# Moving modulation weights out of two feed-forwards into the mixers

## The chip, the cores and the metric

The kernel runs on one core of one Trainium2 chip. The metric is the device time of one execution in microseconds (us), median of several runs. The kernel before takes 2105.08 us (three runs, 2104.85 to 2108.06).

## The reference, cut to what matters

Two transformer blocks of two layers each run one after the other over 256 tokens of width 1024, all in float32. Each layer has a mixer (projections, attention and, in the first block, a state space scan) and a feed-forward (SwiGLU of width 2816, or eight experts). That makes eight stages, numbered m = 0 to 7; stage 3 is the one with the experts. Ahead of each stage its input is shifted and scaled, and behind it the result is gated, by vectors that depend on the condition `c` alone:

```
m = einsum("bd,de->be", silu(c), w) + b          # w: 1024 x 3072 for every stage
shift, scale, gate = split(m, 3)
h = norm(x) * (1 + scale) + shift                # the stage's input
x = x + gate * stage(h)                          # second block; a layer norm around it in the first
```

So each stage needs three thirds (j = 0 shift, 1 scale, 2 gate) of its own 12 MB matrix, and they can be computed at any time before the stage needs them.

## The kernel before, in words

**The ring.** All large weights come in blocks of 1 MB (128 partitions x 2048 floats) through a ring of six slots (`NS = 6`). `plan` is the order of the blocks, 517 in all. The SyncE queue (SP) issues the loads strictly in that order (L2987, `load`), and load n waits until block n - 6, which had the slot before, has been used. A weight block of a stage is split by ScalarE (ACT) into a high half (`high_halves`, L1263, `ring_hi`, three buffers) and by VectorE (DVE) into a low half in the ring slot itself (`low_halves`, L1960, `ring_lo`), and TensorE (PE) makes three products of it (L499 to L501). `ahead(i)` says how far ahead of block i the halves are made: two blocks, but across the border to the next stage only one, the first block of that stage.

**The modulations.** A block `("mod", m, j, p)` is a quarter (p = 0 to 3) of one third. Only DVE uses it: two multiply-adds into `acc` or another accumulator (L1900, `gemv`). DVE takes the quarters off the list `mods_left` in the order of the plan, in `low_halves`, before it makes the low half of the first weight block that stands behind them. `together(m)` adds up shift and scale over the partitions on PE (L550) just before the stage, and takes what is left of them first.

**The order around the change.** `weave` spreads modulation blocks evenly between the blocks of a feed-forward. The first feed-forward (m = 1) carries 32 of them, among them shift and scale of stage 3; the second mixer (m = 2) four; the third mixer (m = 4, `mixer2(0)`) eight, one behind each block from the ninth on; the third feed-forward (m = 5) 28, among them all of stage 7; the last mixer (m = 6, `mixer2(1)`) and the last feed-forward (m = 7) none. "The third feed-forward" is here the one of the second block's first layer, which stands behind the experts.

**The end of a mixer.** A mixer's 16 blocks are 12 of the input projection and four of the output projection, `wout2` 2, 3, 0, 1 in this order. PE uses `wout2` 2 and 3 during the attention, and 0 and 1 in `last_blocks`, whose 48 products end the mixer; the signal that block 0 has been used is given six products before the last. ACT's last steps are `out_block(0)` and `out_block(1)`, and DVE's are `block("wout2", 0)` and `block("wout2", 1)`. The last one makes the halves of the first block of the next feed-forward, `w1 0 0`. Both engines work in order, so only behind it do they come to `rms_rows` and `rms_boundary`: the residual (L2044, L2049), the sum of squares, the normalized rows, which PE transposes (L581) and which give the next stage's input. `mixer1` ends in the same way, with `wout` 2 and 3 taken whole (`whole_block`, L888) and `outputs` (L2371, L2376) and `mixed` (L2037) before it.

Of the kernel before, what the change touches and what calls it, by code (L numbers as in the profile page):

```python
# [87 lines left out]
def hybrid_kernel(nc, a, out):  # L88
    ctx = ExitStack()
    with ctx:  # L90
# [251 lines left out]
        def put_blocks(blocks):  # L342
            for b in blocks:
                block(*b)
# [4 lines left out]
        for i, n in enumerate((0, 1, 1, 1, 1, 2, 2)):  # L349
# [8 lines left out]
                         mods((1, 2), (4, 0), (4, 1), (2, 0), (2, 1), (2, 2), (3, 0), (3, 1))))  # L358
        put_blocks(weave(win_blocks(1) + rowblocks(("wout", 1), a["w_out"][1]), mods((3, 2))))
# [4 lines left out]
        for l in range(2):  # L364
            win2 = [(("win2", l, i), (kview(8, 256), krows(a["w_in_2"][l][:, 256 * i:256 * i + 256]))) for i in WIN2]
            blocks = win2 + rowblocks(("wout2", l), a["w_out_2"][l])
            for i, b in enumerate(blocks):
                put_blocks([b] + (mods((5, 0), (5, 1))[i - 8:i - 7] if l == 0 and i >= 8 else []))
            put_blocks(weave(ffn_blocks((("ffn2", l), a["w_gate_2"][l], a["w_up_2"][l], a["w_down_2"][l])),
                             mods((5, 2), (6, 0), (6, 1), (6, 2), (7, 0), (7, 1), (7, 2)) if l == 0 else []))  # L370

        split = [key for key, _ in plan if key[0] != "mod" and key not in WHOLE]
        turn_of = {key: i for i, key in enumerate(split)}
# [873 lines left out]
        def scalar_program(act):  # L1247
# [335 lines left out]
            def mixer2(l, m):  # L1583
                M = ("m2", l)

                def project(i, dst, *waits, at_once=False):
                    summed(turn_of["win2", l, i])
                    if not at_once:
                        high_halves(main, ahead(turn_of["win2", l, i]))
                    act.wait_ge(*at(*M, "proj", i))  # L1590
                    for z in waits:
                        act.wait_ge(*at(*z))
                    act.activation(dst, R2.of(*M, "proj", i)[:, :].rearrange("p (t c) -> p t c", t=2), ACT.Copy).then_inc(
                        *main.act((*M, "projected", i), ("free", *M, "proj", i)))
# [59 lines left out]
                project(10, vt(2), at_once=True)  # L1654
                values_in(2)
                turn_group(0)
                halves_for(10)
# [220 lines left out]
        def vector_program(dve):  # L1878
# [71 lines left out]
            def low_halves(s, upto):  # L1950

                while done[0] <= upto:
# [8 lines left out]
                    done[0] += 1  # L1961

# [221 lines left out]
            def mixer1(l, m):  # L2184
# [238 lines left out]
                late_features()  # L2423
                outputs()
                mixed(M, range(2), "wout", l, None)
# [3 lines left out]
            def mixer2(l, m):  # L2429
# [120 lines left out]
                mixed(M, range(2), "wout2", l, evac)  # L2550
                block("wout2", 0)
# [557 lines left out]
```

## Time and profile before

| | us |
|---|---|
| median of three runs | 2105.08 |
| lowest, highest | 2104.85, 2108.06 |
| the profiled execution's own time | 2110.58 |
| its span (first to last instruction) | 2108.7 |
| PE busy (share of the span) | 1979.9 (94%) |
| DVE busy | 1673.0 (79%) |
| ACT busy | 1170.4 (56%) |
| mean granted TensorE clock | 0.96 |

The profiled execution is 5.5 us above the median of the runs, and its span is 1.9 us shorter than its time. Differences inside the span can be set against the median as they are. A busy share is a mean over stages that have different limits, so the stages are to be read one by one.

### The profile page before, as it was taken

How to read it: one execution, taken by the hardware profiler on the slowest of the kernel's cores; microseconds unless marked ns; L12 is line 12 of the kernel's file. 1: busy time of each engine (PE TensorE's matmuls, PEld its weight loads, DVE VectorE, ACT ScalarE, POOL GpSimd, SP SyncE). 2: the span in 40 equal slices, each digit the busy share in tenths (PEclk: the TensorE clock that was granted, in tenths of full speed). 3: DMA queues.
4: the chain of work that ended last, by engine and by line, in shares of the span. 5: the costliest groups of instructions: out<-in, count | busy, mean ns of one | idle time of the engine just before them, and what ended most of it. 6: DMA issues, size and time to landing. Idle time of an engine off the chain costs nothing.

```text
span 2108.7 us, 28332 instructions
## 1 busy us (share of the span) xinstructions
PE 1979.9 (94%) x11530; PEld 1713.3 (81%) x11530; DVE 1673.0 (79%) x1753; ACT 1170.4 (56%) x1316; POOL 72.4 (3%) x121
## 2 busy tenths in 40 slices
PE   6989999999799999999999999878899999989999
PEld 6778899886678887887878888668689989869998
DVE  6777889887788998989898888878778886756444
ACT  3544334464567777777777777556444344654432
POOL 6001000000000000000000000000010000000000
PEclk9988999899899999999999999989789998989999
DMA  9754999644499999999999999824359994324552
GB/s 350 267 183 162 349 352 361 215 150 162 166 343 335 352 373 343 341 358 370 324 356 365 361 336 349 310 81 159 120 209 355 353 366 134 121 80 140 180 182 98
DMA packets 251210, 554.37 MB, mean 263 GB/s; under 512 B 10077, under 2 KB 75857, under 8 KB 251073
## 3 DMA queue, kind: packets, MB, share of 16 engines
q1 hardware_dynamic: 247252, 544.13, 72.3%
q0 software_dynamic: 3552, 8.29, 1.2%
q8 instruction: 94, 1.54, 0.3%
q14 instruction: 44, 0.35, 0.1%
q10 hardware_dynamic: 268, 0.07, 0.0%
HBM read 551.40 MB, written 1.05 MB: 262 GB/s over the span
## 4 chain that ended last, share of the span: by engine, by line
PE 75%; DVE 13%; ACT 6%; issue 3%; DMA 3%; SPq 0%; ACTq 0%; DVEq 0%
PE bank L499 22%; PE bank L501 21%; PE bank L500 21%; DVE ring_lo L1960 4%; ACT ring_hi L1263 3%; DVE acc L1900 2%; PE bank L888 1%; PE bank L581 1%; PE bank L550 1%; DMA ring<-in_ffn_w_dram 1%; PE bank L1088 1%; DVE work L2145 1%; DMA ring<-in_w_in_dram 1%; DMA ring<-in_ada_w_dram 1%; PE bank L527 1%
## 5 line engine op out<-in xcount | busy, mean ns | idle before, releaser
L1960 DVE TENSOR_TENSOR ring_lo<-ring,ring_hi 128x2048 fp32r<-128x2048 f32 x417 | 949.5, 2286 | 252.2 <-ACT ring_hi L1263 249.6
L1263 ACT ACTIVATE ring_hi<-ring 128x2048 fp32r<-128x2048 f32 x417 | 794.9, 1913 | 474.3 <-PE bank L501 232.1
L499 PE MATMUL bank<-hh,ring_hi 128*128 128x256 f32 x1152 | 330.3, 287 | 10.4 <-DVE ring_lo L1960 5.6
L500 PE MATMUL bank<-hl,ring_hi 128*128 128x256 f32 x1152 | 328.2, 285 | 0.0
L501 PE MATMUL bank<-hh,ring_lo 128*128 128x256 f32 x1152 | 328.2, 285 | 0.0
L501 PE MATMUL bank<-ring_hi,hl 128*128 128x256 f32 (+2 forms) x768 | 239.1, 311 | 0.0
L499 PEld LDWEIGHTS bank<-hh,ring_hi 128*128 128x128 f32 x1152 | 223.4, 194 | 13.6 <-DVE hl L2024 5.9
L499 PE MATMUL bank<-ring_hi,hh 128*128 128x256 f32 (+2 forms) x672 | 214.2, 319 | 15.6 <-DVE hl L2024 9.2
L499 PE MATMUL bank<-ring_hi,hgh 128*128 128x512 f32 (+1 forms) x576 | 220.4, 383 | 9.0 <-DVE ring_lo L1960 4.0
L500 PEld LDWEIGHTS bank<-hl,ring_hi 128*128 128x128 f32 x1152 | 223.5, 194 | 1.0 <-issue 0.5
L501 PEld LDWEIGHTS bank<-hh,ring_lo 128*128 128x128 f32 x1152 | 223.2, 194 | 0.0
L501 PE MATMUL bank<-ring_hi,hgl 128*128 128x512 f32 (+1 forms) x576 | 216.3, 375 | 0.0
L500 PE MATMUL bank<-ring_lo,hgh 128*128 128x512 f32 (+1 forms) x576 | 216.2, 375 | 0.0
L500 PE MATMUL bank<-ring_lo,hh 128*128 128x256 f32 (+2 forms) x672 | 208.3, 310 | 0.0
L499 PE MATMUL bank<-ring_hi,uh 128*128 128x512 f32 x496 | 199.1, 401 | 7.3 <-DVE ring_lo L1960 6.2
L500 PE MATMUL bank<-ring_lo,uh 128*128 128x512 f32 x496 | 196.5, 396 | 0.0
L501 PE MATMUL bank<-ring_hi,ul 128*128 128x512 f32 x496 | 196.3, 396 | 0.0
L1900 DVE SCALAR_TENSOR_TENSOR acc<-ring,csil,acc 128x1024 f32<-128x1024 f32 x140 | 179.9, 1285 | 13.4 <-DMA ring<-in_ada_w_dram 6.9
L499 PEld LDWEIGHTS bank<-ring_hi,hh 128*128 128x128 f32 x672 | 135.9, 202 | 31.5 <-issue 22.5
L501 PEld LDWEIGHTS bank<-ring_hi,hl 128*128 128x128 f32 x768 | 151.8, 198 | 6.6
L500 PEld LDWEIGHTS bank<-ring_lo,hh 128*128 128x128 f32 x672 | 136.1, 202 | 4.7 <-issue 0.7
L499 PEld LDWEIGHTS bank<-ring_hi,hgh 128*128 128x128 f32 x576 | 108.1, 188 | 34.7 <-issue 5.3
(425 smaller groups left out, 2788.9 us busy)
## 6 DMA issues: line engine op xcount, KB each, us to landing
ring<-in_moe_w_dram SPq DMA_DIRECT2D x264, 1024.0 KB, 5.2
ring<-in_ada_w_dram SPq DMA_DIRECT2D x48, 1024.0 KB, 7.2
ring<-in_w_mod_dram SPq DMA_DIRECT2D x48, 1024.0 KB, 7.2
ring<-in_w_in_dram SPq DMA_DIRECT2D x40, 1024.0 KB, 6.1
ring<-in_ffn_w_dram SPq DMA_DIRECT2D x33, 1024.0 KB, 5.6
ring<-in_w_gate_dram SPq DMA_DIRECT2D x22, 1024.0 KB, 5.0
ring<-in_w_up_dram SPq DMA_DIRECT2D x22, 1024.0 KB, 5.1
ring<-in_w_down_dram SPq DMA_DIRECT2D x22, 1024.0 KB, 5.0
```

Of the source, the lines that this page charges most:

```text
L499: pe.matmul(ps, xh, wh, start=first, stop=False)
L500: pe.matmul(ps, xh, wl, start=False, stop=False)
L501: return pe.matmul(ps, xl, wh, start=False, stop=last)
L527: x = pe.matmul(R2.of("gatesum", 0, h)[:, :], bc(csil[:, 2 * p + k:2 * p + k + 1], [128, 128]), w[:, k, 512 * h:512 * h + 512], start=p == ...
L550: x = pe.matmul(ps[:, 8 * j + i:8 * j + i + 1], sums_at(m, j)[0][:, 128 * i:128 * i + 128], ones[:, 0:1], start=True, stop=True)
L581: x = pe.transpose(ban[kk][:, 256 * i + 128 * t:256 * i + 128 * t + 128], src[:, t, 128 * kc:128 * kc + 128], ident)
L888: x = pe.matmul(Y[t][h][:, :], YT[:, 2 * i + k, 128 * t:128 * t + 128], w[:, c:c + 512], start=first and k == 0, stop=False)
L1088: x = pe.transpose(ps[:, 128 * c:128 * c + 128], U[:, 128 * c:128 * c + 128], ident)
L1263: act.activation(ring_hi[i % NH][:, 0:z], ring[n % NS][:, 0:z], ACT.Copy).then_inc(*s.hi(("hi", home(s, i), i)))
L1900: x = dve.scalar_tensor_tensor(v, w[:, k, :], csil[:, col:col + 1], v, ALU.mult, ALU.add)
L1960: dve.tensor_tensor(ring_lo[n % NS][:, 0:z], ring[n % NS][:, 0:z], hi, ALU.subtract).then_inc(*s.lo(("lo", home(s, i), i)))
L2145: dve.tensor_tensor(S, R.of(*A, "scores", i, c)[:, 0:384], mask, ALU.add).then_inc(*vec(("free", *A, "scores", i, c)))
```

## The change

Three groups of modulation blocks get other places in `plan`. Shift of stage 3 (four blocks) leaves the first feed-forward and goes into the second mixer, shift and scale of stage 7 (eight blocks) leave the third feed-forward and go into the last mixer, and the eight of stage 5 in the third mixer start two blocks later and end with three in a row behind its last block. On DVE, `one_modulation` takes a quarter off the list at a written place: one before and two behind `outputs` of the second mixer, and three before `block("wout2", 0)` in each of the last two. On ACT, the high half of the block two ahead of `win2` 10 is now made before that projection is copied out, as for all other projections. The amount of work is the same.

```diff
         put_blocks(weave(ffn_blocks((("ffn", 0), ...)),
-                         mods((1, 2), (4, 0), (4, 1), (2, 0), (2, 1), (2, 2), (3, 0), (3, 1))))
-        put_blocks(weave(win_blocks(1) + rowblocks(("wout", 1), a["w_out"][1]), mods((3, 2))))
+                         mods((1, 2), (4, 0), (4, 1), (2, 0), (2, 1), (2, 2), (3, 1))))
+        def put_behind(blocks, behind, extra):
+            for i, b in enumerate(blocks):
+                n = behind[i] if i in behind else 0
+                put_blocks([b] + extra[:n])
+                extra = extra[n:]
+        put_behind(win_blocks(1) + rowblocks(("wout", 1), a["w_out"][1]), {0: 1, 2: 1, 4: 1, 9: 3, 11: 2}, mods((3, 2), (3, 0)))
...
-            for i, b in enumerate(blocks):
-                put_blocks([b] + (mods((5, 0), (5, 1))[i - 8:i - 7] if l == 0 and i >= 8 else []))
+            put_behind(blocks, {10: 1, 11: 1, 12: 1, 13: 1, 14: 1, 15: 3}, mods((5 + 2 * l, 0), (5 + 2 * l, 1)))
             put_blocks(weave(ffn_blocks((("ffn2", l), ...)),
-                             mods((5, 2), (6, 0), (6, 1), (6, 2), (7, 0), (7, 1), (7, 2)) if l == 0 else []))
+                             mods((5, 2), (6, 0), (6, 1), (6, 2), (7, 2)) if l == 0 else []))
...
-                project(10, vt(2), at_once=True)
+                project(10, vt(2))
                 values_in(2)
                 turn_group(0)
-                halves_for(10)
...
+            def one_modulation(m):
+                if mods_left and mods_left[0][1] == m:
+                    gemv(mods_left.pop(0))
...
                 late_features()
+                if l:
+                    one_modulation(3)
                 outputs()
+                if l:
+                    one_modulation(3)
+                    one_modulation(3)
                 mixed(M, range(2), "wout", l, None)
...
                 mixed(M, range(2), "wout2", l, evac)
+                for _ in range(3):
+                    one_modulation(5 + 2 * l)
                 block("wout2", 0)
                 block("wout2", 1)
```

The end of the third mixer in the plan, before and after; behind the arrow stands the block that has the ring slot before, whose use the load waits for (the last mixer is the same after the change, with 7 for 5; before, it has no modulations, and its `ffn w1 0 0` stands behind `win2` 4):

```
before: wout2 3 <- win2 4 | mod 5.1.1 | wout2 0 <- win2 5 | mod 5.1.2 | wout2 1 <- wout2 2 | mod 5.1.3 | ffn w1 0 0 <- wout2 3
after:  wout2 3 <- win2 4 | mod 5.0.3 | wout2 0 <- win2 5 | mod 5.1.0 | wout2 1 <- wout2 2 | mod 5.1.1 <- mod 5.0.2
        | mod 5.1.2 <- wout2 3 | mod 5.1.3 <- mod 5.0.3 | ffn w1 0 0 <- wout2 0 | ffn w1 0 1 <- mod 5.1.0 | ffn w3 0 0 <- wout2 1
```

The end of the second mixer after the change:

```
wout 2 | mod 3.2.3 | mod 3.0.0 | mod 3.0.1 | wout 3 | wout 0 | mod 3.0.2 <- wout 2 | mod 3.0.3 <- mod 3.2.3
| wout 1 <- mod 3.0.0 | moe w1 0 0 <- mod 3.0.1
```

## Rows read from the trace of the kernel before

**Rows 1.** By stage, from its first to its last product: us, busy, PEclk, DMA share, GB/s

```profile
188.90:397.40 208.50, 200.53 (x1365) 185.78 (x1365) 181.08 (x142) 81.65 (x68) 7.44 (x11) 0.98 0.86 313
1388.80:1541.70 152.90, 136.59 (x899) 121.69 (x899) 120.51 (x206) 83.57 (x167) 1.44 (x2) 0.90 0.40 138
1554.00:1749.30 195.30, 192.80 (x1327) 179.75 (x1328) 164.76 (x125) 81.77 (x71) 1.44 (x2) 0.98 0.87 318
1758.80:1906.20 147.40, 135.83 (x903) 120.57 (x903) 104.11 (x196) 85.99 (x174) 0.00 (x0) 0.92 0.31 101
1915.70:2104.80 189.10, 189.05 (x1320) 177.48 (x1320) 93.12 (x63) 75.15 (x59) 0.00 (x0) 0.99 0.46 154
```

**Rows 2.** Waits of PE in the first and in the third feed-forward: us, times, longest

```profile
PE bank L499 <- DVE ring_lo L1960: 7.9, 5, 3.3
...
PE bank L499 <- DVE ring_lo L1960: 2.5, 1, 2.5
```

**Rows 3.** The chain that ended last, near the end of the third mixer: start, us, what

```profile
1530.39 5.01 DMA ring<-in_w_gate_dram
```

**Rows 4.** Timeline of the SP queue there (start, us, what)

```profile
1530.39 0.92 SPq L2987 DMA_DIRECT2D ring<-in_w_gate_dram  x2
1540.37 0.37 SPq L2987 DMA_DIRECT2D ring<-in_w_up_dram  x1
```

**Rows 5.** Timeline of ACT and DVE there (start, us, what, [idle before <- releaser])

```profile
1535.42 1.92 ACT L1263 ACTIVATE ring_hi<-ring 128x2048 fp32r<-128x2048 f32 x1 [3.09 <-DMA ring<-in_w_gate_dram]
...
1537.37 2.29 DVE L1960 TENSOR_TENSOR ring_lo<-ring,ring_hi 128x2048 fp32r<-128x2048 f32 x1 [1.79 <-ACT ring_hi L1263]
1539.58 0.69 DVE L2044 TENSOR_TENSOR XN<-bank,gate 128x512 f32<-128x512 f32 x1
```

**Rows 6.** Timeline of PE: the third feed-forward's first product

```profile
1554.03 0.55 PE L499 MATMUL bank<-hh,ring_hi 128*128 128x256 f32 x1 [1.59 <-DVE hl L2024]
```

**Rows 7.** Timelines of DVE, SP and PE at the end of the last mixer

```profile
1897.95 2.29 DVE L1960 TENSOR_TENSOR ring_lo<-ring,ring_hi 128x2048 fp32r<-128x2048 f32 x1 [2.08 <-ACT ring_hi L1263]
1900.16 0.68 DVE L2044 TENSOR_TENSOR XN<-bank,gate 128x512 f32<-128x512 f32 x1
...
1904.89 1.73 SPq L2987 DMA_DIRECT2D ring<-in_w_gate_dram  x2
...
1915.75 0.55 PE L499 MATMUL bank<-hh,ring_hi 128*128 128x256 f32 x1 [1.59 <-DVE hl L2024]
```

**Rows 8.** Third mixer's modulations by line; then the same two steps in both mixers

```profile
L1900 DVE SCALAR_TENSOR_TENSOR acc<-ring,csil,acc 128x1024 f32<-128x1024 f32 x16 | 20.5, 1281 | 0.3
...
1450.45 1.06 PE L967 MATMUL bank<-cst,PT 128*128 128x128 f32 x8 [0.53 <-DVE PT L2182]
...
1491.90 0.87 DVE L2497 TENSOR_SCALAR YT<-bank,pB 128x256 f32<-128x256 f32 x2
...
1820.22 1.06 PE L967 MATMUL bank<-cst,PT 128*128 128x128 f32 x8 [0.54 <-DVE PT L2182]
...
1856.34 0.87 DVE L2497 TENSOR_SCALAR YT<-bank,pB 128x256 f32<-128x256 f32 x2
```

**Rows 9.** Timelines of DVE and PE at the end of the second mixer

```profile
498.68 1.23 DVE L2376 TENSOR_TENSOR YK<-YK,st 128x1024 f32<-128x1024 f32 x1
507.72 2.60 DVE L1900 SCALAR_TENSOR_TENSOR acc<-ring,csil,acc 128x1024 f32<-128x1024 f32 x2
510.24 6.69 DVE L1960 TENSOR_TENSOR ring_lo<-ring,ring_hi 128x2048 fp32r<-128x2048 f32 x3
517.07 0.69 DVE L2044 TENSOR_TENSOR XN<-bank,gate 128x512 f32<-128x512 f32 x1
...
503.33 1.04 PE L581 MATMUL bank<-cst,YK 128*128 128x128 f32 x8
...
512.67 0.47 PE L499 MATMUL bank<-ring_hi,hh 128*128 128x512 f32 x1 [1.43 <-DVE ring_lo L1960]
```

**Rows 10.** Timeline of PE behind the third feed-forward's one stall

```profile
1737.73 0.72 PE L499 MATMUL bank<-ring_hi,PTr 128*128 128x512 f32 x1 [2.47 <-DVE ring_lo L1960]
```

More of the change, by code:

```diff
@@ L1584, in mixer2, with project @@
                 M = ("m2", l)
-                def project(i, dst, *waits, at_once=False):
+                def project(i, dst, *waits):
                     summed(turn_of["win2", l, i])
-                    if not at_once:
-                        high_halves(main, ahead(turn_of["win2", l, i]))
+                    high_halves(main, ahead(turn_of["win2", l, i]))
                     act.wait_ge(*at(*M, "proj", i))
```

## The prediction

> **What bounds the kernel now.** The page comes first: PE is busy in 94% of the span, so the time is PE's work plus the places where PE waits or runs slowly. The table by stage says where those are [rows 1]. The last feed-forward, without modulations, has PE busy in 189.05 of its 189.1 us, at clock 0.99 and DMA share 0.46: that is what 33 weight blocks cost, 5.7 us each. The third feed-forward does the same work with 28 modulation blocks beside it and takes 195.3 us at DMA share 0.87; the first, with 32, takes 208.5 us. So at most 6.2 us are to be had in the third. The waits of PE say what of it is stall: 2.5 us in one wait in the third, 7.9 us in five in the first, all for the low half of a block [rows 2]. The mixers are another thing. They have the DMA share free (0.40 and 0.31), but their PE is idle for 16.3 and 11.6 us [rows 1], on chains through DVE and ACT. Whoever moves loads into the mixers must therefore read the mixer's end, not its DMA share.
>
> There the chain that ended last goes through a load: 5.01 us from the issue of the next feed-forward's first block at 1530.39 to its landing [rows 3, 4]. ACT makes its high half at 1535.42, DVE its low half at 1537.37, and only at 1539.58 does DVE start the first residual [rows 5]. The distance from issue to residual is 9.19 us. From there it is 14.45 us to the feed-forward's first product at 1554.03 [rows 6]. At 1530.39 the load was released by `wout2` 3, whose slot it takes.
>
> **What changes in the ring.** SP issues in the order of the plan, so a late wait holds all loads behind it. With three modulation blocks behind `wout2` 1, the feed-forward's first block takes the slot of `wout2` 0. That block is released six products before the mixer's last one. In the trace this is the release of the load at 1540.37 in the third mixer [rows 4], and of the one at 1904.89 in the last [rows 7]. Before the change the last mixer had this first block long in place: the low half there starts at 1897.95 and the residual at 1900.16 [rows 7].
>
> **The change part by part** (minus is faster).
>
> *First feed-forward, four blocks fewer.* It then has 28 in the same places as the third has today, whose PE stalls for 2.5 us and not 7.9: -5.4 us [rows 2]. After a stall PE runs slowly at first (a product of 0.72 us after the wait of 2.47 [rows 10]); for four stalls fewer I take another -1.1, an estimate. Together -6.5. Bounds: -10, if all waits go and more of the slow products, and -2, if the stalls come from DVE's other work here.
>
> *Second mixer, four blocks more.* The quarter before `outputs` moves its last step from 498.68 + 1.23 = 499.9 to 502.5; PE turns to its transposes only at 503.33 [rows 9], so this one is hidden, with 0.8 us to spare. If that cover goes, it costs up to 2.6. The two behind `outputs` keep DVE until 507.7, where before it took one quarter at 507.72 and the low halves at 510.24 [rows 9]. `wout` 0 is then ready a little sooner, at about 511.3. But `wout` 1 is issued behind a modulation block that waits for `wout` 2, and PE has used that at 503.3, when it turns to the transposes. Three loads in a row from there: 5.0 us for the first [rows 3] and 2.9 for each further (1.05 MB at 318 GB/s over share 0.87, that is 365 GB/s [rows 1]) give a landing at 514.1, or at 517 with the megabyte of layer norm rows that GpSimd loads in this stretch. The high half takes 1.9 and the low half 2.3 [rows 5], so PE has it at 518.3 to 521.2. Today it needs it 12 products after 512.67, at 515.4. The first expert block lands one load later still, and both engines make its halves before the residual: its low half ends at 521.2 to 524.1, and the residual today starts at 517.07 [rows 9]. That is +4.1 to +7.0. I take +6, and +0.5 for the modulation block that DVE now takes before the second projection's low half at the mixer's start: +6.5. Bounds 0 and +10.
>
> *Third mixer, the blocks two places later.* DVE takes five of the eight quarters between two steps that both mixers have: they are 41.45 us apart here (1450.45 to 1491.90) and 36.12 us in the last mixer without modulations (1820.22 to 1856.34) [rows 8]. Five cost 5.3 us, 1.07 each, of 2.6 us of DVE time each (two of 1281 ns [rows 8]). After the change three fall there: -2.1. At the end the load now goes out at 1540.37 instead of 1530.39: +10.0 [rows 4]. The last three quarters land while PE works on the last blocks, and DVE has taken them before the halves of the feed-forward block come; it stands idle there for that load as it is. Moving the high half before `win2` 10 is copied out costs nothing: ACT has room before that copy. Together +7.9; bounds +5 and +10.
>
> *Third feed-forward, eight blocks fewer.* The stall of 2.5 us goes [rows 2], and the slow products behind it [rows 10], 1.6 by estimate: -4.1. Nothing is late next, since the last feed-forward shows PE full at this work [rows 1]. Bounds -6.2 and 0.
>
> *Last mixer, eight blocks more.* Three quarters in its middle at 1.07: +3.2. At its end the load goes out at 1904.89 + 3.2 = 1908.1, the residual follows 9.19 later at 1917.3, and the first product 14.45 after that at 1931.7, where it is 1915.75 today [rows 3 to 7]. That is +16.0 with the 3.2 in it. Bounds +11, if the middle costs nothing and the rest shrinks, and +21, if the three cost their full 7.7.
>
> **Sum:** -6.5 + 6.5 + 7.9 - 4.1 + 16.0 = +19.8 us. On the profiled execution this is 2110.58 + 19.8 = 2130.4; on the median 2105.1 + 19.8 = 2124.9, so **2125 us**.
>
> **Two rules weighed.** (1) The load from issue to landing took 5.01 us [rows 3]. The Trainium skill (DMA: Bandwidth & Descriptors, "Anatomy of one DMA") gives about 2.0 us fixed and the bytes at 436 GB/s, an estimate of 4.4 us for this block, though for another issuing path; by it each late load would be 0.6 us shorter and the sum 1.2 us less. The row is the nearer, and I keep it. (2) In the third feed-forward PE came out of a wait of 2.47 us with a product of 0.72 us [rows 10], which is the clock's lower level, 1.2 of 2.4 GHz. The Trainium skill (TensorE: Matmul & The Clock Gate, "HAM oscillation") says that an array that idles in waits for DMA falls back to half clock and pays again after each gap. It speaks against this change: two mixer ends get longer gaps, and the second mixer gets a stall in the middle of its last blocks. PE already leaves each border of stages slowly (0.55 us for the first product [rows 6, 7]), so I add nothing at the mixers' ends; the rule at its full weight is a rival below.
>
> **The rivals.**
> (a) *The feed-forward's first block is not what the boundary waits for; the freed DMA decides.* If the residual could start when PE has the first sums, the +10.0 and the last mixer's +12.8 go, and -6.5 + 6.5 - 2.1 - 4.1 + 3.2 = -3.0 remains, with the second mixer's cost hidden too -9.5: 2096 us, faster. It decides if the load reaches the ring before about 1535 on the old clock of the third mixer. For it: in the last mixer today nothing waits for that load. Against it: ACT was idle for 3.09 us until exactly this load in the third mixer [rows 5], and the change puts the load behind a later release. Chance 0.07.
> (b) *The same, but the second mixer's end is hidden*: 19.8 - 6.5 = +13.3, 2118 us. For it: the three loads could overlap more than I count. Chance 0.22.
> (c) *Half clock after each new gap*: three gaps (second, third, last mixer), each with some 3 us more of slow products, as much as the slow part of a stage's beginning, gives 19.8 + 9 = +29, 2134 us. For it: the 0.90 and 0.92 of the mixers' clocks [rows 1]. Chance 0.12.
> (d) *The change only shuffles*: gains and losses of some 10 us cancel, within 0.2%. Chance 0.03.
> The forecast has 0.56.
>
> **How the numbers follow.** 0.2% (4 us) is about what a measurement of this kernel can tell from no change. Forecast, (b) and (c) are slower: 0.90 with what lies between them. Rival (a) is faster in all but its weakest form: 0.06. The rest is the same: 0.04. The range of 2111 to 2134 takes in (b) and (c) and the terms' bounds where they don't all fall on one side; all at their ends they would give 0 and +39. It leaves out (a).
>
> **What would show it.** In the profile after: PE's waits in the first feed-forward near 2.5 us and in the third near none; the load of the first feed-forward block at a mixer's end issued about a microsecond before the mixer's last product, 9 us to the residual, and ACT idle before its high half; PE idle for some 10 us more at each of these two ends; in the second mixer a wait of PE of 3 to 6 us for the low half of `wout` 1. The prediction is wrong if the residual starts while the last products run, as it does at 1900.16 today.

## The result, and the profile after

The changed kernel takes 2121.64 us (median of five, 2120.51 to 2128.99) against 2106.38 us for the kernel before, run beside it (five, 2104.85 to 2109.80). The ratio is 1.0076, interval 1.0059 to 1.0093: slower by some 16 us. Forecast were 2125 us in a range of 2111 to 2134.

The profiled execution took 2127.75 us, with a span of 2125.9, and is one of two of the five that took longer (2127.75 and 2128.99; the others took 2120.5 to 2121.6). A second trace of the same kernel, taken later beside other kernels (`after_again`, span 2120.2), stands in the table next to it. A stage runs from its first product to that of the next stage; the column "before" is in us, the others are the differences to it:

| stage | before | after | after_again | predicted |
|---|---|---|---|---|
| up to the first feed-forward | 188.95 | -1.7 | -0.7 | 0 |
| first feed-forward | 217.40 | -6.2 | -6.5 | -6.5 |
| second mixer | 127.02 | +6.6 | +6.3 | +6.5 |
| experts | 855.48 | -0.2 | -0.1 | 0 |
| third mixer | 165.18 | +5.5 | +3.5 | +7.9 |
| third feed-forward | 204.77 | -4.9 | -5.4 | -4.1 |
| last mixer | 156.95 | +16.8 | +13.4 | +16.0 |
| last feed-forward, to the end | 193.00 | +1.3 | +1.1 | 0 |
| span | 2108.7 | +17.2 | +11.5 | +19.8 |

The stages that gained and lost are those of the forecast. The table by stretch of the changed kernel (columns and order of stages as in [rows 1]):

```profile
187.20:389.40 202.20, 199.99 (x1366) 185.81 (x1367) 171.66 (x134) 81.17 (x67) 6.64 (x10) 0.98 0.84 308
1387.30:1536.70 149.40, 137.13 (x899) 122.03 (x899) 116.58 (x201) 80.91 (x162) 1.44 (x2) 0.90 0.37 128
1558.00:1748.30 190.30, 190.30 (x1321) 178.23 (x1322) 143.25 (x105) 81.39 (x68) 1.44 (x2) 0.99 0.79 282
1757.80:1910.30 152.50, 139.75 (x902) 123.77 (x903) 116.73 (x201) 81.89 (x165) 0.00 (x0) 0.89 0.36 125
1931.60:2122.00 190.40, 190.38 (x1320) 178.77 (x1320) 93.07 (x63) 75.10 (x59) 0.00 (x0) 0.98 0.45 153
```

The third feed-forward now has PE busy in every microsecond (190.30 of 190.30; 192.80 of 195.30 in [rows 1]). Between the stretches lies what the page's shares hide: 1536.70 to 1558.00 and 1910.30 to 1931.60, 21.3 us each without a product, where it was 12.3 and 9.5 ([rows 1]: 1541.70 to 1554.00, 1906.20 to 1915.70). PE's waits for low halves in the first feed-forward, to set against [rows 2] (us, times, longest); in the third there are none left:

```profile
PE bank L506 <- DVE ring_lo L1965: 2.2, 2, 1.8
```

The border behind the third mixer: the chain that ended last, then the timelines of the SP queue, ACT, DVE and PE. They answer to [rows 3 to 6].

```profile
1535.33 5.12 DMA ring<-in_w_gate_dram
...
1504.16 22.04 SPq L3004 DMA_DIRECT2D ring<-in_w_mod_dram  x3
1535.33 0.92 SPq L3004 DMA_DIRECT2D ring<-in_w_gate_dram  x2
...
1540.48 1.91 ACT L1270 ACTIVATE ring_hi<-ring 128x2048 fp32r<-128x2048 f32 x1 [13.21 <-DMA ring<-in_w_gate_dram]
...
1530.66 5.31 DVE L1905 SCALAR_TENSOR_TENSOR acc<-ring,csil,acc 128x1024 f32<-128x1024 f32 x4
1542.42 2.29 DVE L1965 TENSOR_TENSOR ring_lo<-ring,ring_hi 128x2048 fp32r<-128x2048 f32 x1 [6.45 <-ACT ring_hi L1270]
1544.63 0.68 DVE L2054 TENSOR_TENSOR XN<-bank,gate 128x512 f32<-128x512 f32 x1
...
1558.00 0.55 PE L506 MATMUL bank<-hh,ring_hi 128*128 128x256 f32 x1 [1.59 <-DVE hl L2034]
```

ACT is idle for 13.21 us, and what ends this is the landing of exactly this block; DVE has finished the three quarters at 1535.97 and idles 6.45. The load goes out 1.2 us before PE's last product (1536.5), and from there to the residual it is 9.30 us. The last mixer shows the same with other starts (compare [rows 7]); here the quarters on DVE end at 1907.9, before the load is even issued:

```profile
1909.00 0.92 SPq L3004 DMA_DIRECT2D ring<-in_w_gate_dram  x2
...
1899.90 8.02 DVE L1905 SCALAR_TENSOR_TENSOR acc<-ring,csil,acc 128x1024 f32<-128x1024 f32 x6
1916.02 2.29 DVE L1965 TENSOR_TENSOR ring_lo<-ring,ring_hi 128x2048 fp32r<-128x2048 f32 x1 [8.11 <-ACT ring_hi L1270]
1918.23 0.68 DVE L2054 TENSOR_TENSOR XN<-bank,gate 128x512 f32<-128x512 f32 x1
...
1931.61 0.55 PE L506 MATMUL bank<-hh,ring_hi 128*128 128x256 f32 x1 [1.59 <-DVE hl L2034]
```

The end of the second mixer, SP, ACT, DVE and PE, beside [rows 9]. `wout` 1 is the load at 498.07:

```profile
495.93 0.88 SPq L3004 DMA_DIRECT2D ring<-in_ada_w_dram  x2
498.07 0.37 SPq L3004 DMA_DIRECT2D ring<-in_w_out_dram  x1
...
509.33 1.91 ACT L1270 ACTIVATE ring_hi<-ring 128x2048 fp32r<-128x2048 f32 x1 [8.05 <-DMA ring<-in_w_out_dram]
...
495.44 5.31 DVE L1905 SCALAR_TENSOR_TENSOR acc<-ring,csil,acc 128x1024 f32<-128x1024 f32 x4
...
504.07 5.31 DVE L1905 SCALAR_TENSOR_TENSOR acc<-ring,csil,acc 128x1024 f32<-128x1024 f32 x4
511.27 2.29 DVE L1965 TENSOR_TENSOR ring_lo<-ring,ring_hi 128x2048 fp32r<-128x2048 f32 x1 [1.90 <-ACT ring_hi L1270]
...
516.65 0.69 DVE L2054 TENSOR_TENSOR XN<-bank,gate 128x512 f32<-128x512 f32 x1 [0.38 <-PE bank L508]
...
504.30 0.47 PE L506 MATMUL bank<-ring_hi,hh 128*128 128x512 f32 x1 [0.66 <-DVE ring_lo L1965]
...
513.71 0.77 PE L506 MATMUL bank<-ring_hi,hh 128*128 128x512 f32 x1 [6.43 <-DVE ring_lo L1965]
514.28 0.63 PE L507 MATMUL bank<-ring_lo,hh 128*128 128x512 f32 x1
...
517.68 0.39 PE L506 MATMUL bank<-ring_hi,hh 128*128 128x512 f32 x1
517.92 0.40 PE L507 MATMUL bank<-ring_lo,hh 128*128 128x512 f32 x1
```

The same products by stretch (columns as in [rows 1]). The granted clock is 0.50 behind the wait of 6.43 us, that is the lower of the clock's two levels, and 1.00 from 517.68 on:

```profile
513.71:517.68 3.97, 3.96 (x9) 3.11 (x10) 3.29 (x3) 0.33 (x2) 0.00 (x0) 0.50 0.01 3
517.68:523.60 5.92, 5.92 (x28) 4.88 (x27) 5.62 (x12) 0.20 (x1) 0.00 (x0) 1.00 0.00 0
```

### The profile page after: what moved, and what is told of

Same layout as the page of the kernel before. It is cut to its first block, busy times and chain, and to the rows that moved or that the text cites. A ratio compares the mean times of both kernels' runs of the same rounds, so it can differ in the third digit from the quotient of the medians.

```text
span 2125.9 us, 28332 instructions
## 1 busy us (share of the span) xinstructions
PE 1978.5 (93%) x11530; PEld 1710.8 (80%) x11530; DVE 1673.0 (79%) x1753; ACT 1170.8 (55%) x1316; POOL 72.2 (3%) x121
## 4 chain that ended last, share of the span: by engine, by line
PE 74%; DVE 12%; ACT 6%; DMA 4%; issue 3%; SPq 0%; ACTq 0%; DVEq 0%
PE bank L506 22%; PE bank L507 22%; PE bank L508 22%; DVE ring_lo L1965 3%; ACT ring_hi L1270 3%; DVE acc L1905 1%; DMA ring<-in_w_in_dram 1%; DMA ring<-in_w_out_dram 1%; PE bank L1095 1%; PE bank L588 1%; DMA ring<-in_ada_w_dram 1%; DVE work L2155 1%; PE bank L895 1%; PE bank L534 1%; DMA ring<-in_ffn_w_dram 1%
```

## The experiments

Each kernel was timed beside the kernel before on the same chip; what is compared is the ratio to it, and a difference in us is this ratio's distance from 1 times the median of the kernel before. The border (us in the table) is the time from the mixer's last product to the feed-forward's first one; the last product's end is taken as the start of the partition sums on PE (L550 or L557), which follow it at once. What lies ahead of the border is called the mixer's own run.

| kernel | ratio, 95% interval | border 3rd mixer | border last mixer |
|---|---|---|---|
| before | 1 | 12.5 | 9.7 |
| after | 1.0076 (1.0059 to 1.0093) | 21.5 | 21.4 |
| after_again | 1.0071 (1.0048 to 1.0093) | 21.4 | 21.6 |
| third_mixer_only | 1.0020 (1.0011 to 1.0029) | 21.5 | 9.7 |
| last_mixer_only | 1.0038 (1.0024 to 1.0053) | 12.5 | 21.5 |
| shift3_only | 1.0003 (0.9991 to 1.0014) | 12.5 | 9.7 |
| high_half_order | 1.0011 (0.9997 to 1.0025) | 12.5 | 8.9 |
| one_place_earlier | 0.9994 (0.9984 to 1.0004) | 14.3 | 12.8 |
| halves_behind_border | 0.9999 (0.9986 to 1.0012) | 15.3 | 13.6 |
| both_remedies | 1.0027 (1.0016 to 1.0037) | 13.3 | 11.2 |
| block_first | 1.0004 (0.9988 to 1.0020) | 16.0 | 13.1 |
| shift3_early | 0.9988 (0.9975 to 1.0001) | 11.3 | 8.9 |
| best_order | 0.9990 (0.9974 to 1.0005) | 16.0 | 13.3 |
| two_borders | 0.9977 (0.9963 to 0.9992) | 14.3 | 8.8 |

### The parts, one at a time

`third_mixer_only`, on the kernel before (with `one_modulation` three times for l = 0):

```diff
-                put_blocks([b] + (mods((5, 0), (5, 1))[i - 8:i - 7] if l == 0 and i >= 8 else []))
+            put_behind(blocks, {10: 1, 11: 1, 12: 1, 13: 1, 14: 1, 15: 3}, mods((5, 0), (5, 1)) if l == 0 else [])
```

> The kernel before with one part of the change alone: the eight quarters in the third mixer start two places later and end with three behind the last block. Theory (late slot): the border behind the third mixer gets later by what the trace of the changed kernel shows for that stage, +5.5 us (the forecast had +7.9), and nothing else moves: 2106.4 + 5.5 = 2112. Rival 1 (the stages are coupled: a quarter less in the middle frees DMA and DVE for what follows, so the border's loss is given back in the next feed-forward): within 0.2% of before, 2103 to 2110. Rival 2 (the forecast's size is right and the changed kernel's other parts hid some of it): 2114.

Measured +4.2 us (interval +2.3 to +6.1). In its trace the border has the full 21.5 us and the mixer's own run is 5.6 shorter than before (1387.22 to 1534.29, before 152.7). So the border costs 9 and the mixer's own run gives back 3.5 (in `after`) to 5.6. Rival 1's "given back in the next feed-forward" is not seen: that stage takes 204.9 us, before 204.8. Rival 2's 2114, 7.6 above, lies outside the interval.

`last_mixer_only`, on the kernel before (with `one_modulation` three times for l = 1, and without (7, 0) and (7, 1) in the third feed-forward):

```diff
+            put_behind(blocks, {10: 1, 11: 1, 12: 1, 13: 1, 14: 1, 15: 3} if l else {i: 1 for i in range(8, 16)},
+                       mods((5 + 2 * l, 0), (5 + 2 * l, 1)))
```

> The kernel before with one part of the change alone: the eight quarters of shift and scale of stage 7 leave the third feed-forward for the last mixer, in the places that the change gives them. Theory (late slot): last mixer +16.8, third feed-forward -4.9 as the changed kernel's stages show, so +11.9: 2106.4 + 11.9 = 2118.3. Rival 1 (the third feed-forward's gain comes from the first block's late start there, not from eight quarters fewer, so here it is not to be had): +16.8, 2123. Rival 2 (the last mixer's loss is mostly a slower clock that the earlier parts of the change bring with them): under +6, 2112 or less.

Measured +8.0 us (the interval is +5.1 to +11.2, so 11.9 lies just outside; the two medians are 10.1 apart). The trace has the third feed-forward at 199.4 (-5.4), the last mixer at 170.2 (+13.3) and the last feed-forward at 194.0 (+1.0): +8.9. Rival 1 falls, the gain of eight quarters fewer is there without the other parts, and without a longer border ahead of it. Rival 2 falls too: the border alone is 11.8 longer, and the mixer's own run 1.5. Of the +16.8 on which the 11.9 rested, 3.4 belong to the profiled execution of the changed kernel and not to the change.

`shift3_only`, on the kernel before (with the three calls in `mixer1`, and without (3, 0) in the first feed-forward):

```diff
+        put_behind(win_blocks(1) + rowblocks(("wout", 1), a["w_out"][1]), {0: 1, 2: 1, 4: 1, 9: 3, 11: 2}, mods((3, 2), (3, 0)))
```

> The kernel before with one part of the change alone: shift of stage 3 leaves the first feed-forward for the second mixer, with the three calls on DVE. Theory: first feed-forward -7.3 and second mixer +6.6 as the changed kernel's stages show, together -0.7: within 0.2% of before, 2105.7. In the profile: one wait of PE of 5 to 7 us for the low half of the last block of the second mixer. Rival 1 (the first feed-forward's gain is noise of the one profiled run; its stalls come back): +6, 2112. Rival 2 (the wait in the mixer is the profiled run's alone): -6, 2100.

Measured +0.6 us (interval -1.9 to +3.0), no difference. The wait of PE in the middle of the last blocks is there, 4.8 us. The first feed-forward takes 211.8 us (-5.6) and the second mixer 132.0 (+5.0): gain and loss cancel, as forecast. The same trace has 4.2 us more in the third feed-forward, which this edit leaves as it was (209.0 us; PE waits 5.9 us for low halves in four waits, where the trace of the kernel before has the one of 2.5). Five other traces with the same 28 quarters there show no such thing (204.5 to 205.0 us), so one trace's figure for a stage can be off by this much.

`high_half_order`, on the kernel before:

```diff
-                project(10, vt(2), at_once=True)
+                project(10, vt(2))
-                halves_for(10)
```

> The kernel before with the one edit on ACT alone: the high half two ahead of `win2` 10 made before that projection is copied out. Theory (ACT has room there): within 0.2% of before, ratio 0.999 to 1.001. Rival (the copy of the projection is on the path of the attention, and 1.9 us of high half ahead of it delay it): +1.9 in each of the last two mixers, ratio 1.0018, which would be part of the changed kernel's loss.

Measured +2.3 us with an interval from -0.6 to +5.3: it holds the theory and the rival's 3.8. In the trace the third mixer takes 152.67 us up to its last product, before 152.69, and the last 149.6 instead of 147.3, with a border of 8.9 instead of 9.7. But `shift3_early` (below), which has neither this edit nor any other in the last mixer, shows the same 149.6 and 8.9, and over the traces without it and without quarters in this mixer the own run goes from 146.4 to 149.6 us. So neither mixer's trace shows a cost of this edit; by the ratio it stays open, between 0 and a few us.

The three parts sum to 12.8 us. `after_again` was run to see whether the whole is more:

> The changed kernel itself again, beside the two others on one chip. Theory: ratio to before 1.0076 with its interval 1.0059 to 1.0093, the sum of its parts (+4.2 +8.0 +0.6 = 12.8 us, 1.0061, as the three runs with one part each gave it) and of what they have together. Rival (the parts are coupled and the first ratio was high): 1.0061 or less.

It is 1.0071, 15.0 us (the medians are 12.8 apart), with an interval from 10.1 to 19.6. That holds the parts' sum of 12.8 and also 15.1, the sum with the 2.3 of `high_half_order`. No coupling between the parts is needed; the intervals would allow some, and the rival of 1.0061 is not excluded.

### The late load

`one_place_earlier`, on the changed kernel:

```diff
-            put_behind(blocks, {10: 1, 11: 1, 12: 1, 13: 1, 14: 1, 15: 3}, mods((5 + 2 * l, 0), (5 + 2 * l, 1)))
+            put_behind(blocks, {9: 1, 10: 1, 11: 1, 12: 1, 13: 1, 14: 1, 15: 2}, mods((5 + 2 * l, 0), (5 + 2 * l, 1)))
-                for _ in range(3):
+                for _ in range(2):
```

> The changed kernel with the eight quarters of each of the last two mixers one place earlier, so that two and not three stand behind the last block; the first block of the next feed-forward then takes the slot of a quarter behind the third-last weight block and goes out as soon as that one has been used. Theory (late slot: the residual waits for the load of that block plus 9.2 us): in the changed kernel's trace the loads freed by that use go out by 1526.2 and 1898.2, the feed-forward block at 1535.33 and 1909.00. The residual should start near 1526.2 + 9.2 + 1.1 = 1536.5 instead of 1544.63, and near 1908.5 instead of 1918.23; some 1 us of each is given back behind it (14.45 us from residual to first product where the wait is short, 13.37 where it is long). Together -7.1 - 8.7 = -15.8: 2121.6 goes to 2106. Rival 1 (the gap at the border costs by itself, through PE's clock and the quarters on DVE, and not through the load): the residual stays where it is, 2121 to 2124, with the quarter in the middle to pay. Rival 2 (the three quarters in a row on DVE, 2.6 us each, are what delays the border): one less saves 2.6 at each border, 2116.

Ratio 0.9994 against 1.0076 of the changed kernel: 0.0082, some 17 us (15.8 forecast), by moving the quarters of two mixers up one place, so that the feed-forward's block takes a slot that is free earlier. By rival 1 nothing would have been gained, and by rival 2 5 us; both fall. SP, ACT and DVE at the third mixer's end:

```profile
1525.45 0.47 SPq L3004 DMA_DIRECT2D ring<-in_w_gate_dram  x1
...
1532.89 1.92 ACT L1270 ACTIVATE ring_hi<-ring 128x2048 fp32r<-128x2048 f32 x1 [5.90 <-DMA ring<-in_w_gate_dram]
...
1534.84 2.29 DVE L1965 TENSOR_TENSOR ring_lo<-ring,ring_hi 128x2048 fp32r<-128x2048 f32 x1 [1.90 <-ACT ring_hi L1270]
1537.05 0.68 DVE L2054 TENSOR_TENSOR XN<-bank,gate 128x512 f32<-128x512 f32 x1
```

The load goes out 9.9 us earlier, and the residual starts 7.6 us earlier, at 1537.05. The expectation of 1536.5 is met within 0.6, though the distance from issue to residual was 11.6 and not 9.2: a quarter goes out 0.4 us ahead of this block, and the block lands 7.4 us after its issue instead of 5.1. DVE's quarters end at 1532.9 here, when ACT is only beginning the high half, so nothing waits for them.

`halves_behind_border`, on the changed kernel: loads and quarters untouched, ACT and DVE make the halves of that block later.

```diff
-                    high_halves(main, ahead(turn_of["wout2", l, i]))
+                    if i != 1:
+                        high_halves(main, ahead(turn_of["wout2", l, i]))
...
                 rms_rows(m + 1, lambda t, h: ("r", m, t, h))
+                high_halves(main, turn_of["ffn2", l, "w1", 0, 0])
                 modulated(m + 1)
...
                 rms_boundary(m, sums_in, lambda t, h: [("Y", "wout2", l, t, h)])
+                low_halves(main, turn_of["ffn2", l, "w1", 0, 0])
                 together(m + 1)
```

> The changed kernel, loads and quarters where it has them, but at the end of the last two mixers ACT and DVE make the halves of the next feed-forward's first block behind the border's own work (residual, squares, normalized rows) and not ahead of it. Theory (the late load holds the border only because both engines work in order and meet its halves first): the residual starts while the last products run, and the first product of the feed-forward comes as long after the mixer's last product as it does in the last mixer of the kernel before, 1915.75 - 1906.2 = 9.55 us, plus 2.3 for the low half: 1536.5 + 11.9 = 1548.4 instead of 1558.0, and 1910.2 + 11.9 = 1922.1 instead of 1931.6. Together -19.1: 2121.6 goes to 2102.5, below the kernel before. Rival 1 (the block itself is late, whoever makes its halves when): the load lands at 1540.45, high and low half after it and all of the border's work stay in a row: 2118 to 2122. Rival 2 (the second block's halves are then late too, and PE stalls behind the first): 3 to 4 us given back at each border, 2109.

Ratio 0.9999: with the load as late as in the changed kernel, the time is that of the kernel before. In this trace the load goes out at 1532.16, 1.2 us before the partition sums start, as in the changed kernel. So the load held the border only through the order of work on two engines. But 6.2 and 7.8 us were won at the borders, where 9.6 and 9.5 were forecast. ACT, DVE and PE show what is in the way:

```profile
1541.53 1.90 ACT L1270 ACTIVATE ring_hi<-ring 128x2048 fp32r<-128x2048 f32 x1
...
1527.56 5.31 DVE L1907 SCALAR_TENSOR_TENSOR acc<-ring,csil,acc 128x1024 f32<-128x1024 f32 x4 [0.19 <-DMA ring<-in_w_mod_dram]
1532.79 0.68 DVE L2056 TENSOR_TENSOR XN<-bank,gate 128x512 f32<-128x512 f32 x1
1543.46 2.29 DVE L1967 TENSOR_TENSOR ring_lo<-ring,ring_hi 128x2048 fp32r<-128x2048 f32 x1 [0.92 <-ACT ring_hi L1270]
1546.01 1.90 DVE L2031 TENSOR_SCALAR hT<-bank,cols 128x256 f32<-128x256 f32 x4
...
1548.65 0.55 PE L506 MATMUL bank<-hh,ring_hi 128*128 128x256 f32 x1 [4.09 <-ACT hT L1325]
```

The residual starts at 1532.79, just before the mixer's last product ends at 1533.33. In the last mixer of the kernel before it starts 5.9 us before that end (1900.16 and 1906.05), and the forecast of 11.9 us for the border took this lead for granted. Here DVE comes to it only behind the last quarters: with the load out of the way, these hold the residual. The last normalized rows are ready at 1542.5, and then DVE waits 0.92 for the high half, makes the low half for 2.29 and only then comes to the stage's input: 3.5 us in the chain where 2.3 were counted. Rival 2's stall behind the first block is not seen; the next feed-forward takes 199.3 us (1548.65 to 1747.99).

`both_remedies`: `one_place_earlier`, and the halves behind the border at all four mixers.

```diff
+            low_halves(main, turn_of["ffn", 0, "w1", 0, 0])     # behind boundary(0, ...); high half behind layer_norm(1)
+            low_halves(main, moe0)                              # behind boundary(2, ...); high half behind layer_norm(3)
```

> The changed kernel with the quarters one place earlier (as in the run one_place_earlier, 2108.3 us, 0.9994 of before) and with the first block's halves made behind the border's work at the end of all four mixers. Theory: the load is no longer late, so only what the halves cost ahead of the border is left to gain: third mixer's border from 1550.45 to about 1535.5 + 11.9 = 1547.4, the last one's by about 2, nothing at the first two mixers, where no engine waits for that load: -5, 2103 against 2108.3, ratio to before 0.997. Rival 1 (with a load in time the halves ahead of the border lie in idle time, and behind it they are on the path, 2.3 us at each of four borders): slower, 2112 to 2117. Rival 2: no difference within 0.2% of one_place_earlier.

Slower than `one_place_earlier` by 0.0033, 7 us: rival 1. In its trace the border behind the first mixer takes 12.4 us (178.62 to 191.02) where `one_place_earlier` has 9.5 (177.51 to 187.00), and the one behind the second 11.2 against 8.1. At the last two the gain was 1.0 and 1.6, so the four borders make up 3.4 of the 7 us; the rest is spread over the stages of this one trace. At the first two borders the halves had lain in idle time ahead of the border, and behind it they are on the path. At the last two little was left for the second remedy to gain. The two are for the same ill and hardly add.

`block_first`: `one_place_earlier`, with the feed-forward's first block ahead of the last two quarters.

```diff
+            quarters = mods((5 + 2 * l, 0), (5 + 2 * l, 1))
+            put_behind(blocks, {9: 1, 10: 1, 11: 1, 12: 1, 13: 1, 14: 1}, quarters[:6])
+            put_blocks(feed[:1] + quarters[6:] + feed[1:])      # feed: the woven feed-forward
```

> The kernel of the run one_place_earlier (2108.3 us, 0.9994 of before) with one thing changed: at the end of the last two mixers the next feed-forward's first block stands ahead of the last two quarters in the order of the loads, not behind them. It then takes the slot of a quarter used long before, and the two quarters take slots that are free by 1526 and 1888 of that run. Theory (only the time at which this load goes out counts): its halves are made before the last products run, the residual starts some 6 us before the mixer's end as in the last mixer of the kernel before, and the feed-forward's first product comes 9.6 to 9.7 us behind the mixer's end instead of 14.25 (1536.20 to 1550.45) and 12.83 (1900.12 to 1912.95). Together -4.6 - 3.2 = -7.8: 2100.5, ratio to before 0.996. Rival 1 (the two quarters then land later than DVE can use them and it waits for them ahead of the last low halves): the gain goes, 0.999 to 1.001. Rival 2 (what is left of the 14.25 and 12.83 are the quarters on DVE, 5.3 us of them there ahead of the border, and not the load): -2 at most, 0.998 to 0.999.

The theory failed as it was put here: 1.0004, and the borders are 16.0 and 13.1 and not 9.6. SP, DVE at the third mixer's end:

```profile
1505.57 0.47 SPq L3006 DMA_DIRECT2D ring<-in_w_gate_dram  x1
1524.37 0.88 SPq L3006 DMA_DIRECT2D ring<-in_w_mod_dram  x2
...
1529.97 5.32 DVE L1907 SCALAR_TENSOR_TENSOR acc<-ring,csil,acc 128x1024 f32<-128x1024 f32 x4 [2.93 <-DMA ring<-in_w_mod_dram]
1535.21 2.28 DVE L1967 TENSOR_TENSOR ring_lo<-ring,ring_hi 128x2048 fp32r<-128x2048 f32 x1
1537.41 0.69 DVE L2056 TENSOR_TENSOR XN<-bank,gate 128x512 f32<-128x512 f32 x1
```

The block is there long before, as wanted. But now the first of the two quarters waits for `wout2` 3, and the second stands behind it: they go out at 1524.37, DVE waits 2.93 us for them, and they, the low half and the residual stand in a row. Rival 1. It isn't one block that must be in time but all that stands ahead of the residual on an in-order engine. The late slot was handed on, not removed.

### The second mixer, and what the runs point to

`shift3_early`, against `shift3_only`:

```diff
-        put_behind(..., {0: 1, 2: 1, 4: 1, 9: 3, 11: 2}, mods((3, 2), (3, 0)))
+        put_behind(..., {0: 1, 2: 1, 4: 1, 6: 1, 7: 1, 8: 1, 9: 2}, mods((3, 2), (3, 0)))
```

> As the run shift3_only (shift of stage 3 in the second mixer instead of the first feed-forward, nothing else changed), but with the eight quarters of the second mixer spread so that no block between the output projection's first and last one takes a slot that is freed late: behind blocks 0, 2, 4, 6, 7, 8 and two behind `wout` 2, none behind `wout` 0. Theory (PE's wait of 4.8 to 6.4 us in the middle of the mixer's last blocks comes from `wout` 1, which stands behind a quarter that waits for `wout` 2): the wait goes, the second mixer takes 127 + 1 to 2 instead of 132 to 134, and the first feed-forward's gain of 7 is kept: ratio to before 0.997 to 0.998. Rival 1 (the wait comes from DVE, which has 7.9 us of quarters to take there): the wait stays, ratio 1.000. Rival 2 (more quarters in the middle cost 1 to 2.6 us each on DVE's chain): ratio 1.000 to 1.002, without the wait.

Ratio 0.9988 (0.9975 to 1.0001), 3.2 us less than `shift3_only`; the two intervals overlap, so it is the trace that carries this. The wait is gone: PE waits 2.3 us for low halves in the whole mixer, the longest 1.7, where the changed kernel has 9.4 and 6.4, as the waits show:

```profile
PE bank L506 <- DVE ring_lo L1967: 2.3, 2, 1.7
```

The mixer takes 129.3 us (397.69 to 527.03), 2.3 above before. Since DVE still takes eight quarters there, rival 1 falls.

`best_order` is `block_first` with this placement:

> The kernel of the run block_first with the second mixer's eight quarters placed as in the run shift3_early. Theory: the two gains are at different borders and add up. shift3_early's second mixer took 129.3 us in the trace where one_place_earlier's took 134.0, so -4.7 on block_first: 2096, ratio to before 0.994. Rival (the second mixer's gain is taken back in the stage of the experts, or the two kernels' runs differ by less than their scatter): ratio as block_first's.

0.9990, 3 us below `block_first` where 4.7 were expected (the intervals overlap), and not 0.994, since `block_first` had failed. `two_borders` keeps what had worked: `shift3_early`, the third mixer as in `one_place_earlier`, and no quarters in the last mixer.

```diff
+            put_behind(blocks, {9: 1, 10: 1, 11: 1, 12: 1, 13: 1, 14: 1, 15: 2}, mods((5, 0), (5, 1)) if l == 0 else [])
```

> The kernel before with two of the three moves, each in the places that the runs point to: shift of stage 3 in the second mixer as in shift3_early (ratio to before 0.9988), and the third mixer's eight quarters as in one_place_earlier, whose trace has that mixer at 163.4 us, from its first product to the next stage's, against 165.2 before; the last mixer stays without quarters. Theory (both borders have their loads in time or no later than before): 0.9988 less 1.8 us, ratio 0.998, 2106 on a before of 2110. Rival (1.8 us in one trace is scatter, or the second mixer's gain is): within 0.2% of before, 0.999 to 1.001.

0.9977 (0.9963 to 0.9992): 2103.96 us beside 2109.55 for the kernel before. It beats both kernels. What each of the two moves gives by itself is less sure: `shift3_early` alone has 0.9988, and the third mixer in the new places takes 164.0 us in this trace, where it took 165.2, and 162.7 in `shift3_early`, where it was not touched.

## Why the prediction was right, point by point

*First feed-forward*, -6.5: -6.2 and -6.5. PE's stalls fell from 7.9 to 2.2 us [rows 2], as forecast from the third feed-forward with the same number of quarters. All traces bear this out: in the four with 32 quarters PE waits 7.9 to 10.2 us for low halves, in the nine with 28 and the old border ahead of them 1.9 to 3.5.

*Second mixer*, +6.5: +6.6 and +6.3. `wout` 1 was the block that came late, and it came nearly when the forecast had it. The forecast's times are on the clock of the kernel before, where this stage starts at 406.35; in the changed kernel it starts at 398.43. Counted from the stage's start:

| | forecast | after |
|---|---|---|
| the quarters behind `wout` 2 go out | 97.0 | 97.5 |
| `wout` 1 has landed | 107.8 to 110.7 | 110.9 |
| its low half is made | 112.0 to 114.9 | 115.1 |
| longest wait of PE | 3 to 6 | 6.4 |
| the residual starts (before: 110.7) | 114.9 to 117.8 | 118.2 |

One step was different: `wout` 1 did not go out in a row with the quarters but 2.1 us behind them, at 498.07, when DVE had used the quarter in its own slot (DVE begins it at 495.44 and needs 2.6 us). The residual thus came 7.5 us later. Two things that I had left out nearly cancel, which is luck: the products behind the wait were slow (1.9 us, below), and from the residual to the experts' first product it took 15.4 us instead of 16.3. `shift3_early` shows that it was the order of the loads, not the number of quarters.

*Third mixer*, +7.9: +5.5, +3.5 and alone +3.3. This is the most mis-sized term. The end was +9.0 for +10.0 forecast. The middle was -4.0 (the two steps of [rows 8] are now at 1448.89 and 1486.38, 37.5 us apart for 41.45) for -2.1. Two of five quarters left it, as forecast, and saved 2.0 each and not 1.07: the forecast had spread the cost of five evenly. The traces show that it isn't even. The two steps are 36.1 us apart without a quarter between them, 37.5 to 38.2 with three, 38.9 with four (both mixers of `one_place_earlier`) and 41.45 with five. In `after_again` the rest of the own run is 1.5 shorter still. The distance from residual to first product shrank from 14.45 to 13.37, since the mixer's last product had ended 8 us before the residual started, and no part of the border's work waited for one.

*Third feed-forward*, -4.1: -4.9 and -5.4, within its bounds. No wait for a low half is left.

*Last mixer*, +16.0: +16.8 and +13.4. The end is +11.8 for +12.8. The middle is +1.8 in both traces (37.9 us between the two steps, 36.12 before [rows 8]) for +3.2, by the same even spreading of the cost. What the first trace has above the second goes with a lower granted clock (below).

*Last feed-forward*, 0: +1.3 and +1.1, with no wait in it. Not forecast and not explained. `last_mixer_only` has it too (194.0 us), but so has `halves_behind_border` (194.3), whose border is short, and `two_borders` has 191.7.

So the mechanism is the forecast's at all three mixers, and the sum of 19.8 was too high (17.2 and 11.5 in the two spans, 16 and 15 in the ratios): the two ends by 1.0 us each and the two middles by 1.9 and 1.4, against which stand the third feed-forward, 0.8 to 1.3 better than its term, and the last one, which was left out. The stages up to the first feed-forward, where nothing was changed, differ by -1.7 and -0.7.

*Rival (a)*, the freed DMA decides: false for this kernel, and yet the right question. `halves_behind_border` is that rival made true, by changing who waits: its two engines do the border's work first, and the 16 us are gone. *Rival (b)*, the second mixer's end is hidden: false, the stage lost 6.6 and 6.3 us. *Rival (c)*, slow products behind the gaps: at one of its three gaps the rows show a price, and it is 1.9 us and not 3. Behind the wait of 6.43 us in the second mixer nine products need from 513.71 to 517.68, 0.44 us each, at a granted clock of 0.50, and from there on they start 0.23 apart at 1.00: 1.9 us, inside the +6.6. The Trainium skill (TensorE: Matmul & The Clock Gate, "HAM oscillation") says that the array pays so after each long gap; for this gap the trace agrees. At the two borders nothing came on top: the third feed-forward takes 199.9 and 199.3 us behind a border of 21.5 us, and 199.4 in `last_mixer_only` behind one of 12.5. *Rival (d)*, the change only shuffles: false, the interval of the ratio begins at 1.0059. *The first rule*: the late load took 5.12 us, near the 5.01 of [rows 3]. The estimate of 4.4 us from the figures of the Trainium skill (DMA: Bandwidth & Descriptors, "Anatomy of one DMA"), which stand there for another issuing path, did not hold here.

## What to carry to other kernels

In a ring of buffers loaded in a fixed order, moving small loads shifts which use every later load waits for; write down, for each load near a border, whose slot it takes and when that is released. Look then for the block that an in-order engine handles ahead of the border's own work: when its load comes late, the border starts late, even if the data are needed much later. A remedy that moves the late slot to another block in the same row of work gains nothing, and two remedies for one wait hardly add. And the cost of small work put into a stage need not be even: here three quarters between two steps cost 1.4 us and five cost 5.3.

## What the runs showed of the hardware

Between the two traces of the changed kernel the two last mixers differ by 2.0 and 3.6 us (149.2 and 152.3 us up to the last product, against 147.2 and 148.8), which is about the whole distance of the two spans (5.7). The granted clock differs there. The stretches are cut at the same distance from the mixer's start; the end of the third, the beginning and the end of the last mixer, first of `after`:

```profile
1500.00:1536.50 36.50, 34.03 (x147) 27.38 (x147) 24.77 (x44) 12.37 (x29) 0.00 (x0) 0.81 0.32 116
...
1757.85:1785.00 27.15, 27.15 (x195) 26.19 (x196) 18.55 (x20) 14.63 (x16) 0.00 (x0) 0.90 0.37 117
...
1870.00:1910.20 40.20, 37.73 (x166) 29.89 (x164) 26.79 (x45) 14.91 (x33) 0.00 (x0) 0.83 0.29 106
```

and of `after_again`, the same kernel:

```profile
1500.45:1534.97 34.52, 31.08 (x148) 25.15 (x148) 24.67 (x44) 12.43 (x30) 0.00 (x0) 0.90 0.33 122
...
1755.74:1782.90 27.16, 26.98 (x213) 25.82 (x214) 19.25 (x21) 16.05 (x19) 0.00 (x0) 1.00 0.39 122
...
1867.90:1904.50 36.60, 33.47 (x157) 26.50 (x156) 24.74 (x44) 13.73 (x32) 0.00 (x0) 0.91 0.32 116
```

At the end of the third mixer the work is the same (147 and 148 PE operations, DVE and ACT busy for the same time), the clock 0.81 against 0.90 and the stretch 2.0 us longer. In the last mixer's first 27 us PE gets through 195 operations at 0.90 and 213 at 1.00. So a quarter of a percent between two executions of one kernel goes here with a lower granted clock in parts of two stages, and a term read from one trace is uncertain by as much. Why the clock was lower in one of them no run here shows.

A load behind others in flight was seen to land later: the block issued 0.4 us behind a quarter in `one_place_earlier` had landed 7.4 us after its issue, where the traces before and after have 5.01 and 5.12 for this block without a quarter just ahead of it. `wout` 1 in the second mixer, 2.1 us behind two quarters and about 1 us behind two loads of GpSimd's, needed 11.3.
